# A two-block transformer forward pass: standardised tokens for router and experts, the norm's scale and bias applied elsewhere

## The chip, the cores and the metric

The kernel runs on one core of one Trainium2 chip. It is written in Bass: each engine has its own instruction stream, and semaphores order the streams. The time is the device time of one execution in microseconds (us), taken as the median of several runs. Lower is better.

## The reference

The program computes two blocks on 256 tokens of width 1024 in fp32. The first (retention, dilated attention, MLP) isn't touched. The second has two layers, and each ends so:

```python
heads = jnp.concatenate([y_a, y_b, y_c], -1)
mix = jnp.einsum('bsc,cd->bsd', heads, w_out[l])
x = _layernorm(DEEPNORM_ALPHA * x + mix, ln1_g[l], ln1_b[l])
ffn = _hier_moe(x, router_group_w[l], router_group_b[l], router_expert_w[l], router_expert_b[l],
                expert_w_gate[l], expert_w_up[l], expert_w_down[l])
x = _layernorm(DEEPNORM_ALPHA * x + ffn, ln2_g[l], ln2_b[l])
```

`_layernorm` subtracts the mean, multiplies by the inverse root of the variance, then by `g`, and adds `b`. The router (4 group logits, 16 expert logits per token, each a product with `x` plus a bias) picks one group and two of its four experts per token. An expert is silu(x w_gate) * (x w_up), weighted, then times w_down.

## The kernel before

Every large fp32 product is three fp32r products: ACT copies a weight unit (128x1024) rounded into `w_hi` (L660), GpSimd or VectorE subtracts to get `w_lo` (L604, L1894), activations are split likewise into `xT_hi`/`xT_lo`, `yT_hi`/`yT_lo`, `xg_hi`/`xg_lo`, and TensorE runs hi*hi, hi*lo, lo*hi (L1136 to L1138). Weights come by SyncE's DMAs into eight raw slots `w_raw`; four slots hold the split form. `unit_used`, `hi_ready` and `lo_ready` count units through these stages.

Each engine's order is written out by hand. In one layer, from the mixed heads on, it is this.

- **Head outputs.** TensorE turns pairs of head columns and multiplies by eight `w_out` units (`down_pairs`, `down_tail4`, L1228 and L1254). VectorE normalises the mLSTM heads in two halves (`centred`, L2558), then the SSD heads, and makes the `yT_lo` remainders (L1888). GpSimd splits the last four units in quarters (L604, 128x256 each), and then the router's unit (L646). `heads_wait` (L1748) holds the third and fourth turn until their heads are ready.
- **Norm.** VectorE adds each half of each 128-token tile (`residual`, L2328), takes statistics (L1930), and normalises in two passes per half (`normed`, L2293): `(x - mean) * g` into PSUM (L2298), then `* rstd + b` back to `x_sb` (L2301). `g` and `b` are rows broadcast to all partitions (`ln1_g`, `ln1_b` in `mod`). TensorE transposes the tile (`turn_x`, L1176), ACT and VectorE split it (L704, L1900).
- **Router.** 16 products of 40 and 20 columns per tile (L1768 to L1771) on the router's unit. VectorE adds the bias row (L2636) and picks groups and experts in a long row of dependent instructions on a few columns, each followed by a drain.
- **Gather.** ACT and VectorE split the normalised tokens untransposed (`xk_hi` L1067, `xk_lo` L2628). TensorE gathers them by one-hot products into four PSUM groups (L1798), transposed and sorted by expert group. ACT (L1072) and VectorE (L2699) split each group. In between VectorE makes `w_lo` of the first expert units, and behind the fourth group the routing weights (`comb`, L2706 to L2718).
- **Experts.** 16 visits. In the first TensorE takes three of four up units, then waits for `comb` (`route_in`) and multiplies it by the one-hots (L1847), and takes the fourth. ACT's silu (L1093) and VectorE's product with the weight (L2731) follow. GpSimd has no work in this stage.
- **Second residual.** VectorE adds the experts' sum to `x_sb` (L2768), so `x_sb` must hold the full normalised rows by then.

Layer 1 repeats this. Weight loads of the router's unit carry 160 columns of use and are padded to 1024.

## Time and profile before

| | us |
|---|---|
| median of 3 runs | 1416.35 |
| lowest, highest | 1414.29, 1416.54 |
| profiled execution, its time | 1416.86 |
| its span, first to last instruction | 1414.5 |
| PE / DVE / ACT / POOL busy | 1312.9 / 856.0 / 735.0 / 639.7 |

The profile is of one execution. Busy time is summed over instructions, and PE's instructions are pipelined, so its 93% isn't peak. DVE is VectorE, POOL is GpSimd, PE is TensorE. The chain follows back from the last instruction to whatever released each step. In a timeline, a bracket gives how long the engine sat idle before the row and whose instruction ended that. An instruction that was issued but had to wait inside its engine shows as a longer instruction, not as idle time.

### The profile page before, as it was taken

What the parts mean: (1) busy time and instruction counts of PE and PEld (TensorE: products, weight loads), DVE (VectorE), ACT (ScalarE), POOL (GpSimd) and SP (SyncE); (2) the same over time, 40 slices, a digit from 0 to 9 for tenths busy, and PEclk for the clock granted to TensorE, in tenths of its full rate; (3) what the DMA queues carried; (4) which work ended last, traced back from release to release, by engine and by line L of the source; (5) the groups of instructions that cost most, each with busy time, mean ns of one, the idle gap of its engine ahead of it and who ended that gap; (6) DMA issues with size and microseconds to landing.
All of it is one profiled execution on the core that took longest, in us unless ns stands there. A gap on an engine that the chain in (4) does not pass through costs nothing.

```text
span 1414.5 us, 17480 instructions
## 1 busy us (share of the span) xinstructions
PE 1312.9 (93%) x6096; PEld 1069.1 (76%) x6096; DVE 856.0 (61%) x1345; ACT 735.0 (52%) x1090; POOL 639.7 (45%) x522
## 2 busy tenths in 40 slices
PE   6899988999999899999998979999989988799996
PEld 3687767888886688887787767888868776788884
DVE  7574763354243543113677667878867857677777
ACT  4343443454464544445566426666646663467664
POOL 2899899988767789998400420000060024000000
PEclk9999999999999999999999879999999989799998
DMA  9966458665443545554531008878754300577782
GB/s 380 367 228 238 149 221 291 242 235 198 160 149 134 169 171 183 194 186 179 194 134 60 1 1 312 296 299 327 279 186 160 119 1 0 221 289 283 287 303 89
DMA packets 44476, 279.86 MB, mean 198 GB/s; under 512 B 5453, under 2 KB 8781, under 8 KB 12014
## 3 DMA queue, kind: packets, MB, share of 16 engines
q1 hardware_dynamic: 37426, 263.82, 50.9%
q10 hardware_dynamic: 6974, 15.05, 2.9%
q8 instruction: 44, 0.72, 0.2%
q14 instruction: 32, 0.26, 0.1%
HBM read 274.66 MB, written 4.19 MB: 197 GB/s over the span
## 4 chain that ended last, share of the span: by engine, by line
PE 69%; DVE 12%; POOL 10%; DVEq 3%; ACT 2%; issue 2%; DMA 2%; ACTq 0%; SPq 0%; POOLq 0%
PE G L1136 11%; PE G L1138 11%; PE G L1137 11%; POOL w_lo L604 10%; PE AC L1136 8%; PE AC L1138 8%; PE AC L1137 8%; DVE mod L1981 1%; DMA w_raw<-w_stream 1%; DVE w_lo L1894 1%; PE T L1251 1%; DVE arena L2481 1%; PE G L1708 1%; PE G L1700 1%; ACT w_hi L660 1%
## 5 line engine op out<-in xcount | busy, mean ns | idle before, releaser
L604 POOL TENSOR_TENSOR w_lo<-w_raw,w_hi 128x512 fp32r<-128x512 f32 (+1 forms) x480 | 612.6, 1309 | 365.8 <-ACT w_hi L660 357.9
L660 ACT ACTIVATE w_hi<-w_raw 128x1024 fp32r<-128x1024 f32 x448 | 470.6, 1056 | 395.1 <-PE G L1138 193.9
L1894 DVE TENSOR_TENSOR w_lo<-w_raw,w_hi 128x1024 fp32r<-128x1024 f32 x230 | 278.5, 1223 | 65.0 <-ACT w_hi L660 57.5
L1136 PE MATMUL AC<-w_hi,yT_hi 128*128 128x512 f32 x464 | 184.0, 397 | 3.4 <-DVE yT_lo L2738 1.9
L1136 PE MATMUL G<-w_hi,xT_hi 128*128 128x512 f32 x432 | 179.6, 416 | 1.9 <-DVE xT_lo L1900 1.9
L1137 PE MATMUL AC<-w_lo,yT_hi 128*128 128x512 f32 x464 | 181.2, 391 | 0.0
L1138 PE MATMUL AC<-w_hi,yT_lo 128*128 128x512 f32 x464 | 181.2, 390 | 0.0
L1137 PE MATMUL G<-w_lo,xT_hi 128*128 128x512 f32 x432 | 173.1, 401 | 0.0
L1138 PE MATMUL G<-w_hi,xT_lo 128*128 128x512 f32 x432 | 173.0, 400 | 0.0
L1136 PE MATMUL G<-w_hi,arena_r 128*128 128x512 f32 x320 | 128.0, 400 | 3.9 <-DVE arena L2731 3.4
L1138 PE MATMUL G<-w_hi,arena_r 128*128 128x512 f32 x320 | 125.1, 391 | 0.0
L1137 PE MATMUL G<-w_lo,arena_r 128*128 128x512 f32 x320 | 124.7, 390 | 0.0
L1981 DVE SCALAR_TENSOR_TENSOR mod<-w_raw,sm,mod 128x1024 f32<-128x1024 f32 x46 | 89.3, 1940 | 45.1 <-DMA w_raw<-w_stream 32.3
L1136 PE MATMUL AC<-w_hi,xT_hi 128*128 128x512 f32 x272 | 111.0, 408 | 5.6 <-POOL w_lo L604 5.5
L1138 PE MATMUL AC<-w_hi,xT_lo 128*128 128x512 f32 x272 | 106.3, 391 | 0.0
L1137 PE MATMUL AC<-w_lo,xT_hi 128*128 128x512 f32 x272 | 106.1, 390 | 0.0
L1136 PEld LDWEIGHTS AC<-w_hi,yT_hi 128*128 128x128 f32 x464 | 88.1, 190 | 23.4 <-POOL w_lo L604 3.2
L1138 PEld LDWEIGHTS AC<-w_hi,yT_lo 128*128 128x128 f32 x464 | 88.0, 190 | 18.5
L1137 PEld LDWEIGHTS AC<-w_lo,yT_hi 128*128 128x128 f32 x464 | 88.2, 190 | 17.4
L1136 PEld LDWEIGHTS G<-w_hi,xT_hi 128*128 128x128 f32 x432 | 84.2, 195 | 19.5 <-DVE xT_lo L1900 2.8
L1138 PEld LDWEIGHTS G<-w_hi,xT_lo 128*128 128x128 f32 x432 | 84.0, 194 | 18.7
L1137 PEld LDWEIGHTS G<-w_lo,xT_hi 128*128 128x128 f32 x432 | 84.4, 195 | 16.4 <-issue 0.2
(446 smaller groups left out, 1778.3 us busy)
## 6 DMA issues: line engine op xcount, KB each, us to landing
w_raw<-w_stream SPq DMA_DIRECT2D x152, 1024.0 KB, 4.9
w_raw<-w_expert SPq DMA_DIRECT2D x96, 1024.0 KB, 5.0
...
```

What stands on the lines that cost most here:

```text
L604: i = pool.tensor_tensor(w_lo[:, k % SLOTS, cols], w_raw[:, raw, cols], w_hi[:, k % SLOTS, cols].bitcast(F32), ALU.subtract)
L660: act.activation(w_hi[:, k % SLOTS, cols], w_raw[:, raw, cols], ACT.Copy).then_inc(hi_ready, 1)
L1136: pe.matmul(out, xh, wh, start=start, stop=False)
L1137: pe.matmul(out, xh, wl, start=False, stop=False)
L1138: return pe.matmul(out, xl, wh, start=False, stop=stop)
L1251: i = pe.transpose(T[:, t, c * P:(c + 1) * P], src[:, t, c * P:(c + 1) * P], ident[:, :])
L1700: i = pe.matmul(G[:, 0, c:c + LDH + 1], lw[:, (2 * h + d) % 4, st, t * P:(t + 1) * P], vaug[:, st, h, 0:LDH + 1], start=st == sts[0], stop ...
L1708: i = pe.matmul(G[:, 1, t * S + h * SP_:t * S + (h + 1) * SP_], sw[:, (2 * h + d) % 4, st, t * P:(t + 1) * P], xdt[:, st, d, h * SP_:(h + ...
L1894: dve.tensor_tensor(w_lo[:, k % SLOTS, :], w_raw[:, k % RAW, :], w_hi[:, k % SLOTS, :].bitcast(F32), ALU.subtract).then_inc(lo_ready, 1)
L1981: dve.scalar_tensor_tensor(m, w_raw[:, raw, :], csil[:, s:s + 1], m, ALU.mult, ALU.add).then_inc(ada_used, 1)
L2481: i = dve.scalar_tensor_tensor(xc[:, c, :], xpad[:, c, k:k + S], cv_w[:, c, k:k + 1], xc[:, c, :], ALU.mult, ALU.add)
```

## The change

- The `ln1_g` and `ln1_b` vectors are put in the router's unit as columns (8 + 8 columns behind the 160 weights). VectorE copies them to `gain_col`, `bias_col`, and multiplies the router's weights by the scale into columns 256 to 415 of the same raw slot; ACT and GpSimd split that.
- TensorE multiplies the broadcast bias column by the router's weights (eight fp32 products of 20 columns), and VectorE adds the result to the router's bias row (`r_bias`).
- The norm ends with one pass per half, `(x - mean) * rstd`. The four residual halves, statistics and `xT_lo` halves stand in a new order.
- TensorE transposes the first tile amid the last output product, and runs the first tile's second router half ahead of the second tile's transposes. ACT makes `xk_hi` of a tile right behind its transposed split.
- Each gathered group gets scale and bias by column: on ACT in the split (two instructions for one), on VectorE by two passes in place in PSUM before the remainder.
- GpSimd makes the full rows of `x_sb`, four instructions of 128x1024 per layer, released by the fourth gathered group's remainder (`t_lo`). The second residual waits for them (`x_full`).

```diff
@@ -148,6 +148,7 @@
 LN_ROWS = 4 * D
+SCALED = 256
@@ -414,6 +418,8 @@
         inv_row = sm[:, 436:452]
+        gain_col, bias_col = sm[:, 336:336 + KC], sm[:, 336 + KC:336 + 2 * KC]
+        r_bias = sm[:, 40:60]
         cosM = sm[:, 368:400].rearrange("p (t n) -> p t n", t=TOK)
@@ -643,8 +649,16 @@
                 pool.wait_ge(hi_ready, n + (L_ROUTER + 1))
-                pool.tensor_tensor(w_hi[:, s, ROUTER:2 * ROUTER], w_raw[:, raw_slot(n + L_ROUTER), 0:ROUTER],
+                pool.wait_ge(router_bias, l + 1)
+                pool.tensor_tensor(w_hi[:, s, ROUTER:2 * ROUTER], w_raw[:, raw_slot(n + L_ROUTER), SCALED:SCALED + ROUTER],
                                    w_hi[:, s, 0:ROUTER].bitcast(F32), ALU.subtract).then_inc(lo_ready, 1)
+
+                pool.wait_ge(ln_rows_loaded, l * 16 + 16)
+                pool.wait_ge(t_lo, l * LT + (T_LAYERS + LT_MOE + UP))
+                for t in range(TOK):
+                    pool.tensor_tensor(x_sb[:, t, :], x_sb[:, t, :], row2["ln1_g"], ALU.mult)
+                    pool.drain()
+                    pool.tensor_tensor(x_sb[:, t, :], x_sb[:, t, :], row2["ln1_b"], ALU.add).then_inc(x_full, 1)
@@ -656,8 +670,11 @@
                 act.wait_ge(unit_used, n + k + 1)
-                cols = slice(0, ROUTER if isinstance(n, int) and n >= U_LAYERS and (n + k - U_LAYERS) % L_UNITS == L_ROUTER else UNIT)
-                act.activation(w_hi[:, k % SLOTS, cols], w_raw[:, raw, cols], ACT.Copy).then_inc(hi_ready, 1)
+                if isinstance(n, int) and n >= U_LAYERS and (n + k - U_LAYERS) % L_UNITS == L_ROUTER:
+                    act.wait_ge(router_scaled, (n + k - U_LAYERS) // L_UNITS + 1)
+                    act.activation(w_hi[:, k % SLOTS, 0:ROUTER], w_raw[:, raw, SCALED:SCALED + ROUTER], ACT.Copy).then_inc(hi_ready, 1)
+                else:
+                    act.activation(w_hi[:, k % SLOTS, :], w_raw[:, raw, :], ACT.Copy).then_inc(hi_ready, 1)
@@ -1062,14 +1079,16 @@
                     turn_hi_x(t + (LT_X2 + 2 * tk), tk)
-                for tk in range(TOK):
                     act.wait_ge(x2_ready, HALVES * (l * TOK + (tk + 1)))
...
                     act.wait_ge(t_ready, t + (LT_MOE + q + 1))
-                    act.activation(xg_hi[:, 2 * q:2 * q + 2, :], AC[:, q, :].rearrange("p (c n) -> p c n", n=S), ACT.Copy).then_inc(t_hi, 1)
+                    for c in (2 * q, 2 * q + 1):
+                        i = act.activation(xg_hi[:, c, :], AC[:, q, c % 2 * S:(c % 2 + 1) * S], ACT.Identity, bias=bias_col[:, c:c + 1],
+                                           scale=gain_col[:, c:c + 1])
+                    i.then_inc(t_hi, 1)
@@ -1236,6 +1255,8 @@
                     for c in range(SLOTS):
+                        if j == 1 and c == 2:
+                            amid()
                         i = down_step(n, k, c, c, 1, (j,), False, c == SLOTS - 1)
@@ -1251,7 +1272,7 @@
-            def down_pairs(n, k, t, src, pairs, before=None, tail=True, tail4=False):
+            def down_pairs(n, k, t, src, pairs, before=None, tail=True, tail4=None):
@@ -1745,15 +1766,30 @@
+                def router_biases(c0, c1):
+
+                    raw = raw_slot(n + L_ROUTER)
+                    pe.wait_ge(raw_landed[raw // PIECE], (raw_round(n + L_ROUTER) + 1) * 16)
+                    for c in range(c0, c1):
+                        at = ROUTER + KC + c
+                        i = pe.matmul(G[:, 0, 0:ROUTER // KC], w_raw[:, raw, at:at + 1].to_broadcast([P, P]),
+                                      w_raw[:, raw, c * ROUTER // KC:(c + 1) * ROUTER // KC], start=c == 0, stop=c == KC - 1)
+                    return i
+
                 def heads_wait(q):
+                    if q == 2:
+                        pe.wait_ge(lnum_out, l * LH + LH)
+                        router_biases(0, KC // 2)
+                    if q == 3:
+                        router_biases(KC // 2, KC).then_inc(router_bias, 1)
                     if q >= 2:
...
-                down_pairs(n, L_OUT, tb + LT_OUT, lambda q: HB[:, :, q * 256:(q + 1) * 256], 4, heads_wait, tail4=True)
+                down_pairs(n, L_OUT, tb + LT_OUT, lambda q: HB[:, :, q * 256:(q + 1) * 256], 4, heads_wait,
+                           tail4=lambda: turn_x(tb + LT_X2, 0, x_sb, x2_ready, HALVES * l * TOK))
...
-                turn_x(tb + LT_X2, 0, x_sb, x2_ready, HALVES * l * TOK)
                 pe.wait_ge(lo_ready, n + (L_ROUTER + 1))
@@ -1774,8 +1810,8 @@
                 pe.wait_ge(t_lo, tb + (LT_X2 + 2))
+                router(0, range(KC // 2, KC))
                 turn_x(tb + (LT_X2 + 2), 1, x_sb, x2_ready, HALVES * (l * TOK + 1))
-                router(0, range(KC // 2, KC))
                 pe.wait_ge(t_lo, tb + (LT_X2 + 3))
@@ -2586,6 +2622,12 @@
                 down_los(tb + LT_OUT, 0, 1)
+                raw = raw_slot(n + L_ROUTER)
+                dve.wait_ge(raw_landed[raw // PIECE], (raw_round(n + L_ROUTER) + 1) * 16)
+                dve.tensor_copy(sm[:, 336:336 + 2 * KC], w_raw[:, raw, ROUTER:ROUTER + 2 * KC])
+                dve.tensor_tensor(w_raw[:, raw, SCALED:SCALED + ROUTER].rearrange("p (c n) -> p c n", c=KC),
+                                  w_raw[:, raw, 0:ROUTER].rearrange("p (c n) -> p c n", c=KC),
+                                  w_raw[:, raw, ROUTER:ROUTER + KC].unsqueeze(2).to_broadcast([P, KC, ROUTER // KC]), ALU.mult).then_inc(router_scaled, 1)
                 centred(2, LH)
@@ -2614,26 +2656,41 @@
                 down_los(tb + LT_OUT, 2, 4)
-                for t in range(TOK):
+                dve.wait_ge(router_bias, l + 1)
+                dve.tensor_tensor(r_bias, G[:, 0, 0:ROUTER // KC], row2["router_b"], ALU.add)
+
+                def summed(t, c):
+                    acc_wait(l * LACC + ACC_LAYERS, n + done(L_ROUTER), t, c)
+                    residual(t, c)
+                    stats_half(t, c)
+
+                def standard(t):
+
+                    inverse_root(r + 4 + t, t)
                     for c in range(HALVES):
-                        acc_wait(l * LACC + ACC_LAYERS, n + done(L_ROUTER), t, c)
-                        residual(t, c)
-                        stats_half(t, c)
-                    ln_var(t)
-                    if t == 0:
-                        dve.wait_ge(ln_rows_loaded, l * 16 + 16)
-                    normed(r + 4 + t, t, "ln1_g", "ln1_b", x2_ready, (lambda: lo_x(tb + LT_X2, 0)) if t == 1 else None)
+                        dve.tensor_scalar(x_sb[:, t, half(c)], x_sb[:, t, half(c)], mv[:, t, 0:1], var[t], ALU.subtract, ALU.mult).then_inc(x2_ready, 1)
+
+                summed(0, 0)
+                summed(0, 1)
+                ln_var(0)
+                standard(0)
+                summed(1, 0)
+                lo_x_half(tb + LT_X2, 0, 0)
+                summed(1, 1)
+                ln_var(1)
+                lo_x_half(tb + LT_X2, 0, 1)
+                standard(1)
                 def token_lo(t):
...
+                token_lo(0)
                 lo_x(tb + (LT_X2 + 2), 1)
-                token_lo(0)
                 token_lo(1)
...
                 nr = EGROUPS + EXPERTS
-                dve.tensor_tensor(rlog, AC[:, 0:TOK, 0:nr], wide(row2["router_b"]), ALU.add)
+                dve.tensor_tensor(rlog, AC[:, 0:TOK, 0:nr], wide(r_bias), ALU.add)
                 dep()
@@ -2696,6 +2753,10 @@
                     dve.wait_ge(t_hi, tb + (LT_MOE + q + 1))
+                    for c in (2 * q, 2 * q + 1):
+                        gathered = AC[:, q, c % 2 * S:(c % 2 + 1) * S]
+                        dve.tensor_scalar(gathered, gathered, gain_col[:, c:c + 1], bias_col[:, c:c + 1], ALU.mult, ALU.add)
+                    dep()
                     dve.tensor_tensor(xg_lo[:, 2 * q:2 * q + 2, :], AC[:, q, :].rearrange("p (c n) -> p c n", n=S),
@@ -2765,6 +2826,7 @@
                         dve.wait_ge(acc_ready, l * LACC + (ACC_LAYERS + 3 + HALVES * t + c + 1))
+                        dve.wait_ge(x_full, l * TOK + t + 1)
                         residual(t, c)
@@ -2830,7 +2892,9 @@
         router = np.concatenate([a["router_group_w_2"][l], we], axis=1)
-        parts.append(padded(router.reshape(KC, P, -1).transpose(1, 0, 2).reshape(1, P, -1), UNIT))
+        affine = np.concatenate([a[k][l].reshape(KC, P).T for k in ("ln1_g_2", "ln1_b_2")], axis=1)
+        router = np.concatenate([router.reshape(KC, P, -1).transpose(1, 0, 2).reshape(P, -1), affine], axis=1)
+        parts.append(padded(router[None], UNIT))
     units = np.concatenate(parts, axis=0).reshape(-1, RAW, P, UNIT)
```

VectorE's order in the norm, before (`x_sb` the tokens, `sm` the statistics, `AC` and `T` PSUM):

```order
L2298 SCALAR_TENSOR_TENSOR AC<-x_sb,sm,mod 128x512 x2
L1947 RECIPROCAL sm<-sm 128x1
L2301 SCALAR_TENSOR_TENSOR x_sb<-AC,sm,mod 128x512 x2
L2328 SCALAR_TENSOR_TENSOR x_sb<-x_sb,AC 128x512
L1930 BN_STATS sm<-x_sb 128x6
L2328 SCALAR_TENSOR_TENSOR x_sb<-x_sb,AC 128x512
L1930 BN_STATS sm<-x_sb 128x6
L1935 BN_AGGR sm<-sm 128x2
L2333 TENSOR_SCALAR sm<-sm 128x1
L1900 TENSOR_TENSOR xT_lo<-T,xT_hi 128x4x128 x2
```

and now:

```order
L2369 TENSOR_SCALAR sm<-sm 128x1
L1983 RECIPROCAL sm<-sm 128x1
L2671 TENSOR_SCALAR x_sb<-x_sb,sm 128x512 x2
L2364 SCALAR_TENSOR_TENSOR x_sb<-x_sb,AC 128x512
L1966 BN_STATS sm<-x_sb 128x6
L1936 TENSOR_TENSOR xT_lo<-T,xT_hi 128x4x128
L2364 SCALAR_TENSOR_TENSOR x_sb<-x_sb,AC 128x512
L1966 BN_STATS sm<-x_sb 128x6
L1971 BN_AGGR sm<-sm 128x2
L2369 TENSOR_SCALAR sm<-sm 128x1
L1936 TENSOR_TENSOR xT_lo<-T,xT_hi 128x4x128
```

Two passes per tile through PSUM are one pass in place, and the first tile's `xT_lo` halves stand apart, the first of them ahead of the second tile's last residual.

VectorE's order behind the second gathered group, before (`w_lo<-w_raw,w_hi` an expert unit's remainder, `arena_r<-AC` a group's, `sm` the routing weights):

```order
L2699 TENSOR_TENSOR arena_r<-AC,arena_r 128x512
L1894 TENSOR_TENSOR w_lo<-w_raw,w_hi 128x1024
L2699 TENSOR_TENSOR arena_r<-AC,arena_r 128x512
L1894 TENSOR_TENSOR w_lo<-w_raw,w_hi 128x1024 x2
L2706 TENSOR_REDUCE sm<-sm 128x2
L2707 TENSOR_SCALAR sm<-sm 128x2
L2709 TENSOR_TENSOR sm<-sm 128x2
L2711 RECIPROCAL sm<-sm 128x2
L2712 TENSOR_TENSOR sm<-sm 128x8
L2714 TENSOR_TENSOR sm<-sm 128x8
L2716 TENSOR_TENSOR sm<-sm 128x8
L2718 TENSOR_TENSOR sm<-sm 128x32
```

and now:

```order
L1930 TENSOR_TENSOR w_lo<-w_raw,w_hi 128x1024
L2758 TENSOR_SCALAR AC<-AC,sm 128x256 x2
L2760 TENSOR_TENSOR arena_r<-AC,arena_r 128x512
L1930 TENSOR_TENSOR w_lo<-w_raw,w_hi 128x1024
L2758 TENSOR_SCALAR AC<-AC,sm 128x256 x2
L2760 TENSOR_TENSOR arena_r<-AC,arena_r 128x512
L1930 TENSOR_TENSOR w_lo<-w_raw,w_hi 128x1024 x2
L2767 TENSOR_REDUCE sm<-sm 128x2
L2768 TENSOR_SCALAR sm<-sm 128x2
L2770 TENSOR_TENSOR sm<-sm 128x2
L2772 RECIPROCAL sm<-sm 128x2
L2773 TENSOR_TENSOR sm<-sm 128x8
```

A pair of scalar passes stands ahead of each group's remainder; the units and the routing weights follow as before.

GpSimd's order at the same place, before:

```order
L639 TENSOR_TENSOR arena<-arena 128x256 x2
L639 TENSOR_TENSOR arena<-arena 128x128 x2
L639 TENSOR_TENSOR arena<-arena 128x256
L604 TENSOR_TENSOR w_lo<-w_raw,w_hi 128x256 x16
L646 TENSOR_TENSOR w_hi<-w_raw,w_hi 128x160
L604 TENSOR_TENSOR w_lo<-w_raw,w_hi 128x256 x32
```

and now:

```order
L610 TENSOR_TENSOR w_lo<-w_raw,w_hi 128x256 x16
L653 TENSOR_TENSOR w_hi<-w_raw,w_hi 128x160
L659 TENSOR_TENSOR x_sb<-x_sb,mod 128x1024
L661 TENSOR_TENSOR x_sb<-x_sb,mod 128x1024
L659 TENSOR_TENSOR x_sb<-x_sb,mod 128x1024
L661 TENSOR_TENSOR x_sb<-x_sb,mod 128x1024
L610 TENSOR_TENSOR w_lo<-w_raw,w_hi 128x256 x32
```

Between the router's unit and the next layer's first eight units stand four instructions on whole rows.

## Rows read from the trace of the kernel before

**Rows 1.** Page: busy us (share) xinstructions; the chain that ended last, by engine.

```profile
PE 1312.9 (93%) x6096; PEld 1069.1 (76%) x6096; DVE 856.0 (61%) x1345; ACT 735.0 (52%) x1090; POOL 639.7 (45%) x522
...
PE 69%; DVE 12%; POOL 10%; DVEq 3%; ACT 2%; issue 2%; DMA 2%; ACTq 0%; SPq 0%; POOLq 0%
```

**Rows 2.** VectorE timeline: start, duration (us), engine, line, out<-in, xcount [idle before].

```profile
800.10 0.85 DVE L1888 TENSOR_TENSOR yT_lo<-T,yT_hi 128x256 fp32r<-128x256 f32 x2 [2.97 <-ACT yT_hi L672]
...
801.62 0.76 DVE L2571 TENSOR_TENSOR arena<-arena,sm 128x256 f32<-128x256 f32 x2
...
805.87 0.17 DVE L1916 TENSOR_SCALAR sm<-sm 128x8 f32<-128x8 f32 x1
```

**Rows 3.** Timeline of GpSimd, then of TensorE, the output product's stretch.

```profile
807.38 13.93 POOL L604 TENSOR_TENSOR w_lo<-w_raw,w_hi 128x256 fp32r<-128x256 f32 x16 [13.60 <-ACT w_hi L660]
...
809.25 0.66 PE L1251 MATMUL T<-ident,arena 128*128 128x128 f32 x4 [1.17 <-DVE arena L2599]
...
821.37 0.50 PE L1136 MATMUL AC<-w_hi,yT_hi 128*128 128x512 f32 x1 [0.23 <-POOL w_lo L604]
```

**Rows 4.** Timeline of VectorE, norm of both tiles and router.

```profile
825.61 1.41 DVE L2298 SCALAR_TENSOR_TENSOR AC<-x_sb,sm,mod 128x512 f32<-128x512 f32 x2
...
830.59 0.69 DVE L1930 BATCH_NORM_STATS2 sm<-x_sb 128x6 f32<-128x512 f32 x1
...
831.71 1.28 DVE L1900 TENSOR_TENSOR xT_lo<-T,xT_hi 128x512 fp32r<-128x512 f32 x2
...
834.46 1.41 DVE L2301 SCALAR_TENSOR_TENSOR x_sb<-AC,sm,mod 128x512 f32<-128x512 f32 x2
...
842.24 0.20 DVE L2636 TENSOR_TENSOR sm<-AC,mod 128x40 f32<-128x40 f32 x1 [1.00 <-PE AC L1771]
```

**Rows 5.** Timeline of TensorE: small fp32 products, then the turning of both tiles.

```profile
780.08 1.45 PE L1708 MATMUL G<-arena 128*128 128x64 f32 x12
...
828.31 1.03 PE L1176 MATMUL T<-ident,x_sb 128*128 128x128 f32 x8
...
835.32 1.94 PE L1176 MATMUL T<-ident,x_sb 128*128 128x128 f32 x8 [1.74 <-issue]
```

**Rows 6.** Windows: stretch, us, busy by engine, granted clock, DMA share, GB/s.

```profile
834.00:836.00 2.00, 0.69 (x4) 0.72 (x5) 1.80 (x4) 0.00 (x0) 0.00 (x0) 0.55 0.00 0
854.00:855.00 1.00, 1.00 (x8) 1.00 (x8) 0.74 (x2) 0.90 (x2) 0.00 (x0) 0.66 0.97 410
```

**Rows 7.** VectorE groups by shape: line, op, shapes xcount | busy us, mean ns.

```profile
L2679 DVE TENSOR_SCALAR xT_lo<-arena,sm 128x256 fp32r<-128x256 f32 x4 | 1.2, 350 | 0.2
...
L2421 DVE COPY arena<-arena 128x512 f32<-128x512 f32 x2 | 0.9, 428 | 0.1
```

**Rows 8.** Timeline of VectorE, then of TensorE: gather and first visit.

```profile
854.87 1.23 DVE L1894 TENSOR_TENSOR w_lo<-w_raw,w_hi 128x1024 fp32r<-128x1024 f32 x1 [0.26 <-ACT w_hi L660]
...
861.95 0.19 DVE L2718 TENSOR_TENSOR sm<-sm 128x32 f32<-128x32 f32 x1
...
864.44 0.96 PE L1847 MATMUL T<-sm,xT_lo 128*128 128x16 f32 x8
...
870.33 0.47 PE L1136 MATMUL G<-w_hi,arena_r 128*128 128x512 f32 x1 [1.69 <-DVE arena L2731]
```

**Rows 9.** Timeline of GpSimd at 509 and 1051 us, of VectorE at 522 and 814.

```profile
509.82 13.52 POOL L604 TENSOR_TENSOR w_lo<-w_raw,w_hi 128x512 fp32r<-128x512 f32 x10 [0.17 <-ACT w_hi L660]
524.35 2.55 POOL L604 TENSOR_TENSOR w_lo<-w_raw,w_hi 128x512 fp32r<-128x512 f32 x2 [1.00 <-ACT w_hi L660]
...
1051.81 11.38 POOL L604 TENSOR_TENSOR w_lo<-w_raw,w_hi 128x256 fp32r<-128x256 f32 x16 [6.04 <-ACT w_hi L660]
...
522.22 1.18 DVE L2267 SCALAR_TENSOR_TENSOR sm<-sm 128x32 f32<-128x32 f32 x1
523.47 0.18 DVE L2269 TENSOR_SCALAR sm<-sm 128x32 f32<-128x32 f32 x1
...
814.02 0.69 DVE L2612 TENSOR_TENSOR arena<-arena,sm 128x512 f32<-128x512 f32 x1
```

7 lines of the change are left out of this document (5 added, 2 removed).

## The prediction

> **What bounds the kernel now.** I read the page first. TensorE (PE) is busy 93% of the span and carries 69% of the chain that ended last; VectorE (DVE) and GpSimd (POOL) carry 12% and 10% [rows 1]. The change touches only the two layers of the second block, so I read the timelines of layer 0 from 799 to 872 us, engine by engine; layer 1 shows the same rows 368.4 us later. Three stretches matter.
>
> *Head outputs.* DVE runs without a gap from 800.1 us to the variance of 805.87 [rows 2]. The ACT root waits for that, the conversion of the next weights stands behind the root, POOL's sixteen pieces wait for the conversion and start at 807.38, and PE waits 0.23 us for them at 821.37 [rows 3]. So a delay of DVE here passes to PE.
>
> *Norm and router.* DVE spends 1.41 us on each of two passes per tile [rows 4]. PE ends the output product near 828.3 and then mostly waits: it turns the first tile at 828.31, the second only at 835.32 [rows 5], and DVE gets the router's logits at 842.24 [rows 4]. The granted clock is 1.00 (2.4 GHz) until inside 834 to 836 us (0.55 there), and is back only inside 854 to 855 us, some 5 us after PE's work became dense again at 849.5 [rows 6]. The fall comes about 5 us after the dense products ended; layer 1 does the same.
>
> *Gather and first visit.* DVE is still choosing experts when the first gathered group is ready, and PE's first expert product waits for DVE's unit of 854.87. The routing weights are ready at 862.14 (861.95 plus 0.19), PE asks for them at 864.44 and has passed on by then; PE next waits at 870.33, for DVE's hidden product [rows 8]. From about 875 us to the end of the stage PE is full, so any delay up to there stays.
>
> **The change, part by part, for one layer.**
>
> 1. Two DVE instructions for the router unit: a copy of 16 columns and a product of 160. They stand in the DVE run above. Two 256-column products take 0.76 us together [rows 2], 0.38 for each step; 160 columns come to about 0.28, the copy to 0.08. Bounds 0.2 and 0.6; I take **+0.35 us**, all on the path.
>
> 2. Eight small matmuls for the bias on PE, four before the third turn and four before the fourth. PE is idle for 1.17 us before the third turn [rows 3] and nearly as long before the fourth, and both gaps grow by 0.35. Six fp32 products of 64 columns take 1.45 us at full clock (12 records [rows 5]), 0.24 each; these have 20 columns, so four take at most 0.97: **0**. If that cover were gone they would cost up to 1.7. The 20-column addition of the bias lies in DVE's wait before 822.4: 0.
>
> 3. The norm. Four passes of 0.7 us per tile and half (1.41 and 1.41 per tile [rows 4]) become one scalar-pair pass per half. No 512-column pass with two scalar columns shows alone. The nearest rows are a 512-column copy within SBUF of 0.43 us and a 256-column scalar pass of 0.35 [rows 7]; the passes of now, 0.7, are the other end. I take 0.54, which is 0.35 plus the extra columns at the copy's pace, and 0.45 per step. The Trainium skill ("VectorE: DVE Perf Modes", Mode 2×_2P) lets a one-source fp32 pass within SBUF move two elements a cycle, and the copy's 0.43 us agrees; by it alone the pass is 0.43, and the sum changes by 0.2 us.
>
>    Tile 0 is then standardised at 827.2, in time for PE, which turns it between two products. That adds 1.0 us of transposes before PE's last product: its end moves from 828.3 to about 829.5. DVE's last half then goes: residual and statistics 1.45 (0.75 and 0.7 [rows 4]), aggregation and variance 0.5, one xT_lo half 0.6 (two take 1.28), reciprocal 0.2, two passes 1.0, giving 833.2 instead of 835.87 (834.46 plus 1.41). PE has done the first tile's router products by then. It turns tile 1 by 834.0, still at full clock by the fall seen [rows 6]. ACT and DVE need 1.1 to 1.6 more; the sixteen router products at half clock need 3.4. The logits come at about 838.65 instead of 842.24: -3.6, and with the 0.35 above **-3.2 us**. Bounds: -1.8 (clock falls before the transposes) and -5.3 (it stays up through the router). The token copies and remainders hide beside PE.
>
> 4. The gather. On DVE each of four groups gets two 256-column passes on PSUM, near 0.37 a step like the pairs of 0.75 to 0.85 [rows 2]: +0.75 each. The first unit for PE is ready 0.9 us later (two groups, less some 0.6 of waits for ACT that vanish, 0.26 of it before the unit [rows 8]), and the fourth group is done 2.6 us later. ACT's two halves in place of one cost 0.15 each and hide. **+0.9 us** if nothing else happens: the weights would be ready at 864.75 and PE would ask at 865.3.
>
> 5. POOL's full rows: four products and sums of 128x1024, released by DVE's fourth group, at about 861.05. POOL is free until the next layer, so its own time costs nothing. What it does to DVE is the main term. In rows 9, ten POOL instructions of 512 columns run back to back from 509.82 to 523.34. Beside them dependent DVE instructions on 32 columns take 1.17 us each; when POOL stops, the same instruction takes 0.18 (523.47). So a DVE instruction that reads two SBUF tensors, or passes SBUF to SBUF with scalars, waits for one whole POOL instruction, and the two engines alternate. This agrees with the Trainium skill ("SBUF — State Buffer", which calls the shared port pair an exclusive lock, held for the whole instruction).
>
>    The new instructions are four times as wide as the 256-column ones. 256 columns take 0.71 us and 512 take 1.275 [rows 9], 0.565 per 256, so 1024 take 2.4 us. Bounds of the hold: 1.3 (no longer than 512 columns) and 2.7. Behind POOL's start DVE has in its queue the third and fourth w_lo units and the eight tiny weight instructions. After the third unit POOL gets in four times: before the fourth unit, and before three of the tiny ones. I take 9.2 us of waits: weights at 864.75 + 9.2 = 873.95. The three last tiny steps run free, included in that.
>
>    **Who waits:** PE stands between the third and fourth unit of the first visit until the weights come. It would have gone on at 864.44; now at 873.95: **+9.5 us** (this contains the 0.9 of point 4; the slack of 0.55 is used up). PE was then idle for 8.7 us, more than the 5 us after which the clock fell, and comes back at half clock for some 5 us, as at 849.5 [rows 6]. That costs up to 2.4 us before the hidden product. I take **+2.0**. DVE's next three units and ACT's silu are ready beside that. From there PE is the limit again and nothing is given back.
>
> 6. The wait for the full rows before the second residual is some 150 us later: 0. The other moves (ACT's token copies, tile 1 turned behind the router products) are inside point 3.
>
> Sum for one layer: -3.2 + 9.5 + 2.0 = +8.3 us; for two +16.6. Against the profiled execution (1416.86 us, its span 1414.5) that is 1433.5. The median of the runs is 0.5 lower, so I say **1433 us**.
>
> **The rivals.**
>
> *A, the row work hides (faster).* If DVE and POOL do not exclude each other here, only points 1 to 4 count: -3.2 + 0.9 = -2.3 a layer, -4.6 in all, **1411.8 us**. For it: POOL has no other work then, and one product with a broadcast operand (814.02) ran at its usual 0.69 us while POOL worked. Against it: the tiny instructions of rows 9 are of the very kinds that stand in this queue. It decides by whether the fourth group's successors lengthen.
>
> *B, the other order of turns.* DVE gets both w_lo units through before POOL's first instruction. Then one turn of POOL falls behind the weights: weights at 871.5, then DVE's next unit waits, and the hidden product comes 9.5 us late instead of 11.5. -3.2 + 9.5 = +6.3, **1429.0 us**. Against it: the paired rows at full load show POOL coming in between.
>
> *C, half the holds.* If POOL holds 1.3 us for each turn, or only two turns fall before the weights, they cost about 4.8 instead of 9.2 us and PE's idle time is too short to lower the clock for long: 9.5 - 4.4 = +5.1, less 3.2, +1.9 a layer, **1420 us**. With the clock also kept up in the router it is zero to slightly faster.
>
> *D, the clock stays up through the router.* PE has router products until 830.5 and again from 832.1, more than before, so the fall may come later. Point 3 is then -5.3; with the holds in place +6.2 a layer, **1429 us**.
>
> **How the numbers follow.** About 0.2% (2.8 us) is what a measurement of this kernel tells from none. Main course 0.48, B 0.14, D 0.10, all slower; C 0.15, of which 0.07 slower, 0.06 within and 0.02 faster; A 0.13, of which 0.12 faster and 0.01 within. Slower 0.79, same 0.07, faster 0.14. The top of the range is a hold of 2.7 us for each of four turns and the whole 2.4 for the clock: about +11.5 a layer, 1439. The bottom leaves out A and the faster part of C: 1415. Between them lies some 0.83.
>
> **What the profile of the changed kernel would show.** DVE's w_lo unit behind the fourth group at 2.5 to 3.5 us instead of 1.22, and two or three of the tiny weight instructions at 2.3 us instead of 0.17 (point 5). POOL's four row instructions at 2.4 us or a little more, spread over 10 to 12 us. A wait of PE of 8 to 9 us before the small products for the weights, with a granted clock of 0.50 after it. In the norm, passes of 0.43 to 0.7 us, logits 3 us earlier counted from PE's last head product, and PE's wait for POOL there unchanged near 0.2. I am wrong if the w_lo units stay at 1.22 while POOL works: then it is A. I am wrong in size if the holds are much shorter than 2.4 us, or if PE's stall is there and the clock is not lowered.

## The result

Over six runs each the changed kernel takes 1432.78 us (median) against 1414.51 us before, a ratio of 1.0137 with a 95% interval of 1.0115 to 1.0159: slower by 19.4 us (16.3 to 22.5). The forecast was 1433.

The page of the changed kernel, busy time and chain by engine, as [rows 1]:

```profile
PE 1321.5 (92%) x6128; PEld 1075.8 (75%) x6128; DVE 866.8 (60%) x1359; ACT 737.7 (51%) x1098; POOL 662.1 (46%) x530
...
PE 67%; DVE 13%; POOL 10%; DVEq 3%; ACT 2%; DMA 2%; issue 2%; SPq 0%; ACTq 0%; POOLq 0%
```

TensorE's share of the chain falls by two points though it has a little more to do: it waits. Three rows of its timeline in layer 0 show where. The first is its first expert product. The second is the place: it answers to the row at 864.44 in [rows 8]. The third answers to 870.33 there:

```profile
857.23 0.50 PE L1155 MATMUL G<-w_hi,arena_r 128*128 128x512 f32 x1 [1.43 <-DVE w_lo L1930]
...
873.96 1.89 PE L1883 MATMUL T<-sm,xT_lo 128*128 128x16 f32 x8 [8.07 <-DVE sm L2779]
...
882.27 0.47 PE L1155 MATMUL G<-w_hi,arena_r 128*128 128x512 f32 x1 [1.69 <-DVE arena L2792]
```

What VectorE does meanwhile (timeline, columns as in [rows 2]), and GpSimd's four new instructions:

```profile
859.91 1.00 DVE L2758 TENSOR_SCALAR AC<-AC,sm 128x256 f32<-128x256 f32 x2
860.99 0.69 DVE L2760 TENSOR_TENSOR arena_r<-AC,arena_r 128x512 fp32r<-128x512 f32 x1
861.59 4.55 DVE L1930 TENSOR_TENSOR w_lo<-w_raw,w_hi 128x1024 fp32r<-128x1024 f32 x2
866.07 0.15 DVE L2767 TENSOR_REDUCE sm<-sm 128x2 f32<-128x8 f32 x1
866.14 2.24 DVE L2768 TENSOR_SCALAR sm<-sm 128x2 f32<-128x2 f32 x1
868.45 2.21 DVE L2770 TENSOR_TENSOR sm<-sm 128x2 f32<-128x2 f32 x1
870.74 0.17 DVE L2772 RECIPROCAL sm<-sm 128x2 f32<-128x2 f32 x1
870.82 2.32 DVE L2773 TENSOR_TENSOR sm<-sm 128x8 f32<-128x8 f32 x1
873.22 0.17 DVE L2775 TENSOR_TENSOR sm<-sm 128x8 f32<-128x8 f32 x1
...
861.82 3.24 POOL L659 TENSOR_TENSOR x_sb<-x_sb,mod 128x1024 f32<-128x1024 f32 x1 [31.98 <-DVE arena_r L2760]
865.21 3.14 POOL L661 TENSOR_TENSOR x_sb<-x_sb,mod 128x1024 f32<-128x1024 f32 x1
868.32 2.33 POOL L659 TENSOR_TENSOR x_sb<-x_sb,mod 128x1024 f32<-128x1024 f32 x1
870.79 2.34 POOL L661 TENSOR_TENSOR x_sb<-x_sb,mod 128x1024 f32<-128x1024 f32 x1
```

An addition to two columns (L2768) takes 2.24 us, and a product of two columns (L2770) 2.21, thirteen times the 0.17 of the reciprocal behind it. The two engines take turns: DVE's second unit waits for POOL's first instruction, and three tiny DVE instructions each wait for one of the others. The reduction does not wait, though POOL is at work beside it (866.07). The reciprocal (870.74) falls where POOL passes from its third instruction to its fourth, so whether it would wait is not shown.

The norm, second tile (timelines of VectorE and TensorE, as [rows 4] and [rows 5]):

```profile
834.36 1.00 DVE L2671 TENSOR_SCALAR x_sb<-x_sb,sm 128x512 f32<-128x512 f32 x2
...
841.93 0.20 DVE L2693 TENSOR_TENSOR sm<-AC,sm 128x40 f32<-128x40 f32 x1 [1.36 <-PE AC L1807]
...
835.76 1.97 PE L1195 MATMUL T<-ident,x_sb 128*128 128x128 f32 x8
```

Windows of the changed kernel, in the norm and in the wait and restart (columns as in [rows 6]):

```profile
834.00:836.00 2.00, 1.74 (x9) 1.74 (x10) 1.92 (x5) 0.00 (x0) 0.00 (x0) 0.64 0.00 0
870.00:872.00 2.00, 0.00 (x0) 0.00 (x0) 1.93 (x3) 0.00 (x0) 1.86 (x2) 0.50 0.23 94
878.00:880.00 2.00, 2.00 (x9) 1.59 (x8) 0.00 (x0) 0.00 (x0) 0.00 (x0) 0.77 0.89 377
```

The two rows of the kernel before from which I count, first residual and first gather instruction on VectorE, and the latter of the changed kernel:

```profile
822.37 0.69 DVE L2328 SCALAR_TENSOR_TENSOR x_sb<-x_sb,AC 128x512 f32<-128x512 f32 x1 [4.41 <-PE AC L1138]
...
852.92 0.69 DVE L2699 TENSOR_TENSOR arena_r<-AC,arena_r 128x512 fp32r<-128x512 f32 x1
```

```profile
852.60 0.55 DVE L2758 TENSOR_SCALAR AC<-AC,sm 128x256 f32<-128x256 f32 x1
```

To compare kernels I measure the stage from starts of rows, so that nothing ahead of it enters: from VectorE's first residual to the logits (the 128x40 addition), from there to the first gather instruction on VectorE, and from that one to three points: TensorE's first expert product, the end of the routing weights, and VectorE's hidden product of the first visit. Microseconds, layer 0 / layer 1:

| kernel | residual to logits | logits to gather | gather to first product | to weights | to hidden |
|---|---|---|---|---|---|
| before | 19.87 / 19.87 | 10.68 / 10.66 | 3.23 / 3.24 | 9.22 / 9.22 | 16.39 / 16.39 |
| after | 17.31 / 17.07 | 10.67 / 10.62 | 4.63 / 4.64 | 21.30 / 21.30 | 28.65 / 28.92 |
| one column | 16.29 / 17.54 | 10.67 / 10.62 | 4.63 / 4.64 | 12.78 / 12.79 | 17.99 / 19.40 |
| before plus rows | 19.86 / 19.86 | 10.69 / 10.33 | 3.23 / 2.94 | 17.59 / 17.50 | 25.23 / 25.31 |
| rows late | 17.56 / 17.03 | 10.65 / 10.61 | 4.64 / 4.64 | 12.78 / 12.78 | 17.99 / 17.99 |
| quarters | 16.27 / 16.28 | 10.66 / 10.62 | 4.64 / 4.63 | 15.46 / 15.48 | 23.67 / 20.74 |
| dense wait | 17.54 / 16.29 | 10.67 / 10.62 | 4.64 / 4.63 | 21.47 / 21.44 | 26.82 / 26.77 |
| late, dense norm | 14.64 / 14.64 | 10.67 / 10.62 | 4.63 / 4.64 | 12.77 / 12.78 | 17.96 / 18.01 |
| late, plain gather | 16.30 / 17.55 | 10.67 / 10.31 | 3.24 / 3.23 | 9.22 / 9.22 | 16.43 / 16.40 |
| gather reordered | 15.82 / 14.65 | 10.66 / 10.61 | 2.95 / 2.96 | 12.78 / 12.78 | 19.41 / 19.39 |
| before, dense norm | 18.10 / 18.11 | 10.69 / 10.65 | 3.23 / 3.13 | 9.22 / 9.12 | 16.44 / 16.33 |
| before, all edits | 18.11 / 18.10 | 10.69 / 10.65 | 2.28 / 2.63 | 9.23 / 9.58 | 14.54 / 14.81 |
| before, fills | 19.86 / 19.86 | 10.69 / 10.66 | 3.13 / 3.05 | 10.53 / 10.46 | 16.29 / 16.21 |
| unit 3 first | 14.63 / 14.64 | 10.68 / 10.62 | 2.96 / 2.96 | 12.78 / 12.79 | 16.38 / 16.39 |

(With one column, layer 1 reads 19.40: the clock fell right behind the wait ahead of the first product there, at about 1218.9, and was back at 1222.)

From residual to hidden product a layer is 46.94 us before and 56.63 after: +9.69, and +0.34 in the heads ahead of it, so about 20 us in two layers. That is the measured difference, within its interval. The profiled execution itself took 1438.42 us, the slowest of the six, and its span is 22.1 us longer than the one before; the other 2 us stand almost all ahead of layer 0's heads (800.10 before, 802.01 after), in code that the change doesn't touch.

### The profile page after: what moved, and what is told of

It reads as the page before. It is cut to its first block, busy times and chain, and to the rows that moved or that the text cites. A ratio compares the mean times of both kernels' runs of the same rounds, so it can differ in the third digit from the quotient of the medians.

```text
span 1436.6 us, 17600 instructions
## 1 busy us (share of the span) xinstructions
PE 1321.5 (92%) x6128; PEld 1075.8 (75%) x6128; DVE 866.8 (60%) x1359; ACT 737.7 (51%) x1098; POOL 662.1 (46%) x530
## 4 chain that ended last, share of the span: by engine, by line
PE 67%; DVE 13%; POOL 10%; DVEq 3%; ACT 2%; DMA 2%; issue 2%; SPq 0%; ACTq 0%; POOLq 0%
PE G L1155 11%; PE G L1157 10%; PE G L1156 10%; POOL w_lo L610 10%; PE AC L1155 8%; PE AC L1157 8%; PE AC L1156 8%; DMA w_raw<-w_stream 2%; DVE mod L2017 2%; DVE w_lo L1930 1%; PE T L1272 1%; DVE arena L2517 1%; PE G L1721 1%; PE AC L1616 1%; PE G L1729 1%
## 5 line engine op out<-in xcount | busy, mean ns | idle before, releaser
L1930 DVE TENSOR_TENSOR w_lo<-w_raw,w_hi 128x1024 fp32r<-128x1024 f32 x230 | 282.5, 1242 | 61.9 <-ACT w_hi L677 54.3
L2017 DVE SCALAR_TENSOR_TENSOR mod<-w_raw,sm,mod 128x1024 f32<-128x1024 f32 x46 | 82.1, 1784 | 42.2 <-DMA w_raw<-w_stream 32.8
```

What stands on the lines that cost most here:

```text
L1930: dve.tensor_tensor(w_lo[:, k % SLOTS, :], w_raw[:, k % RAW, :], w_hi[:, k % SLOTS, :].bitcast(F32), ALU.subtract).then_inc(lo_ready, 1)
L2017: dve.scalar_tensor_tensor(m, w_raw[:, raw, :], csil[:, s:s + 1], m, ALU.mult, ALU.add).then_inc(ada_used, 1)
```

## Experiments

Time differences are the measured ratio times the median of the kernel before in the same call, with the 95% interval.

**One column.** Is it GpSimd's work, or the new arithmetic?

```diff
-pool.tensor_tensor(x_sb[:, t, :], x_sb[:, t, :], row2["ln1_g"], ALU.mult)
+pool.tensor_tensor(x_sb[:, t, 0:1], x_sb[:, t, 0:1], row2["ln1_g"][:, 0:1], ALU.mult)
...
```

The addition behind it is cut to one column in the same way.

> The changed kernel, with GpSimd's four row instructions of a layer cut from 1024 columns to one; the scale and bias of the other columns of the residual rows are left out of the computation. Everything else of the change stays. Theory (VectorE and GpSimd wait for each other's whole instructions at the router's end): VectorE's waits of 2.35 us fall away, the expert weights are ready about 9 us earlier, TensorE's clock stays up. Left over are +0.34 (heads), -2.56 (norm and router) and about +1.4 (gather) a layer, so -0.8 a layer: about 1413 us, between -4 and +1 us against the kernel before. Rival (the new gather, the two scalings or the normalisation cost the time themselves and GpSimd's work is beside it): the time stays above 1425 us, at least +10 us against before.

Measured: -0.6 us (-4.9 to +3.7). The row that took 2.24 us is gone from VectorE's timeline, and GpSimd's instructions wait in turn for VectorE's (1.03 us for one column, 0.19 once VectorE's wide units are over). Timelines of this kernel:

```profile
859.20 0.16 DVE L2768 TENSOR_SCALAR sm<-sm 128x2 f32<-128x2 f32 x1
...
857.09 1.03 POOL L659 TENSOR_TENSOR x_sb<-x_sb,mod 128x1 f32<-128x1 f32 x1 [30.95 <-DVE arena_r L2760]
...
859.22 0.19 POOL L659 TENSOR_TENSOR x_sb<-x_sb,mod 128x1 f32<-128x1 f32 x1
```

All of the loss goes with the width of those four instructions.

**The same instructions in the kernel before**, with nothing else of the change:

```diff
+for t in range(TOK):
+    pool.tensor_tensor(HB[:, t, :], x_sb[:, t, :], row2["ln1_g"], ALU.mult)
+    pool.drain()
+    pool.tensor_tensor(HB[:, t, :], HB[:, t, :], row2["ln1_b"], ALU.add).then_inc(x_full, 1)
...
```

> The kernel before, with four GpSimd instructions of 128x1024 a layer at the place where the changed kernel has them; their results go to scratch and are used by nobody. Nothing else of the change is in it. Lock theory: four waits of 2.3 us on VectorE put the expert weights 9.2 us later, at 871.3 on the scale of the first layer, of which TensorE had 2.3 in hand (864.44), so 6.9 us of stall, and about 2.4 us for a TensorE clock that falls in the stall: about +9.3 a layer, +18.5 in all, 1433 us. Rival (the loss of the changed kernel is in its gather and norm): within 2 us of the kernel before.

Measured: +18.4 us (10.4 to 26.3). Weights 8.37 us later, hidden product 8.84. VectorE and TensorE there:

```profile
853.69 4.57 DVE L1902 TENSOR_TENSOR w_lo<-w_raw,w_hi 128x1024 fp32r<-128x1024 f32 x2
...
858.25 2.27 DVE L2715 TENSOR_SCALAR sm<-sm 128x2 f32<-128x2 f32 x1
...
865.91 1.89 PE L1855 MATMUL T<-sm,xT_lo 128*128 128x16 f32 x8 [5.95 <-DVE sm L2726]
```

So the four instructions are enough by themselves. That both kernels lose the same by them, while the rest of the change nets to nothing, is what these two runs show together.

**Quarters.** Does a wait last as long as one instruction?

```diff
+for a in range(0, D, D // 4):
+    pool.tensor_tensor(x_sb[:, t, a:a + D // 4], x_sb[:, t, a:a + D // 4], row2["ln1_g"][:, a:a + D // 4], ALU.mult)
...
```

> The changed kernel with each GpSimd row instruction cut in four of 256 columns, same place, same amount of work. If a VectorE instruction waits for one whole GpSimd instruction and the two take turns: seven to eight short VectorE instructions wait 0.6 to 0.7 us each, 4.6 us in the place of 9.2, and the clock falls for a shorter time: 1420 to 1424 us. If the wait is for all of GpSimd's work in a row (it does not let VectorE in between), it stays at 1431 to 1435 us. If the holds are shorter than GpSimd's gaps, under 1418 us.

Measured: +7.5 us (3.4 to 11.7), 1421.29. The same DVE rows as above, of this kernel:

```profile
856.02 2.90 DVE L1933 TENSOR_TENSOR w_lo<-w_raw,w_hi 128x1024 fp32r<-128x1024 f32 x2
...
858.90 0.63 DVE L2771 TENSOR_SCALAR sm<-sm 128x2 f32<-128x2 f32 x1
```

The waits are 0.4 to 0.55 us in place of 2.1: they shrink with the length of one GpSimd instruction. Six waits put the weights 2.7 us later than with the rows late, less than the 4.6 expected: presumably part of a GpSimd instruction's 0.7 us has passed when VectorE asks. In layer 0 TensorE waited 2.24 us for the weights and the clock fell behind that (0.50 from 863 to 869 us). In layer 1, where the clock had fallen earlier and slowed the first products, it waited 0.82 us and the clock stayed up until 1241.7, behind the hidden product. So it is 23.67 against 20.74 us to the hidden product, for the same 15.5 to the weights: 2.9 us for where the clock falls.

**Dense wait.** What is the clock's part? TensorE fills its wait with 36 products into a bank that nobody reads; "dense products" below are such products too.

```diff
+pe.wait_ge(lo_ready, n + (L_MOE + UP))
+for spare in range(36):
+    pe.matmul(T[:, 1, :], xg_hi[:, 0, 0:P], w_hi[:, (L_MOE + UP - 1) % SLOTS, 0:NT], start=True, stop=True)
 pe.wait_ge(route_in, l * 4 + 4)
```

> The changed kernel, with 36 products of 128x512 on TensorE (into a bank that nobody reads) at the place where it waits for the expert weights, 36 x 0.23 = 8.3 us, so that the wait of 8.07 us is filled and the clock does not fall in it. The wait itself stays. If the clock's fall costs what the forecast said (2.0 to 2.4 us a layer), the time is 4 to 5 us below the changed kernel's, 1427 to 1429 us. If the clock costs nothing on the path (rival: VectorE's three operands at 874 to 877 and ScalarE set the pace of the restart), it stays within 1 us of the changed kernel's +19 us over before.

Measured: 1428.22 us, +15.1 (9.5 to 20.8) over before. The intervals of this run and of the changed kernel overlap, so the stage decides: hidden product after 26.82 / 26.77 instead of 28.65 / 28.92, that is 1.8 and 2.15 us less, although the spare products hold TensorE 0.5 us longer than the weights do (they are ready at 868.61, TensorE goes on at 869.08). With that 0.5 the clock's fall costs 2.3 and 2.6 us. The products on TensorE:

```profile
860.75 8.50 PE L1882 MATMUL T<-w_hi,arena_r 128*128 128x512 f32 x36 [0.33 <-DVE w_lo L1933]
```

The window behind the wait is at 1.00 here. In the changed kernel, which runs 5.7 us later by its first residual, the clock is at 0.50 from 869 to 878 us, in the wait and behind it:

```profile
870.00:872.00 2.00, 2.00 (x13) 1.70 (x13) 2.00 (x3) 0.00 (x0) 0.00 (x0) 1.00 0.00 0
```

**Rows late.** GpSimd's rows behind hidden tiles of the visits, one at a time:

```diff
 for t in range(TOK):
+    pool.wait_ge(ffn_h, l * VISITS + FF_TILES + 4 * t + 4)
     pool.tensor_tensor(x_sb[:, t, :], x_sb[:, t, :], row2["ln1_g"], ALU.mult)
     pool.drain()
+    pool.wait_ge(ffn_h, l * VISITS + FF_TILES + 4 * t + 6)
```

> The changed kernel with the same four GpSimd instructions moved behind the expert products, one behind every second hidden tile of the visits, where VectorE has idle time. The full computation. Theory: in the visits VectorE is waited for with room, so each 2.3 us hold is hidden, and the time is that of the kernel with one column: about 1413 us, -4 to +1 us against before. Rival (a hold costs wherever it falls, since VectorE's accumulations are needed in time by TensorE there too): four holds of 2.3 us a layer, up to +9 us a layer, 1420 to 1432 us.

Measured: +0.7 us (-3.2 to +4.7). The hold is still there: four units of VectorE take 6.84 us where a row of four without GpSimd takes 5.10 (at 885.28), and nobody waits for them. Timelines of VectorE and GpSimd:

```profile
893.69 6.84 DVE L1932 TENSOR_TENSOR w_lo<-w_raw,w_hi 128x1024 fp32r<-128x1024 f32 x4
...
893.90 3.28 POOL L660 TENSOR_TENSOR x_sb<-x_sb,mod 128x1024 f32<-128x1024 f32 x1 [69.35 <-DVE arena L2794]
```

**Late rows, plain gather**: the above with the gather of before.

```diff
-for c in (2 * q, 2 * q + 1):
-    gathered = AC[:, q, c % 2 * S:(c % 2 + 1) * S]
-    dve.tensor_scalar(gathered, gathered, gain_col[:, c:c + 1], bias_col[:, c:c + 1], ALU.mult, ALU.add)
...
```

> The changed kernel with GpSimd's rows late, and with the gather of the kernel before: the scale and bias of the gathered rows are left out of the computation (one copy on ScalarE, no scaling on VectorE). It measures the gather alone, and by what is left the gain of norm and router. Theory: the gather cost +1.4 us a layer, norm and router gave -2.2 together with the heads: about 3 us below the run with the rows late, 4.4 us below before, 1408 to 1411 us. Rival (the gather's extra VectorE work hides behind TensorE, whose first product waits for something else): same as with the rows late, 1413 us.

Measured: -4.1 us (-6.5 to -1.6). The scale and bias of the gathered rows are left out here. The three columns behind the first gather instruction return to those of before, to 0.04 us. So the new gather costs 1.40 us to the first product and 1.6 to the hidden product, and what norm and router gain is real.

**Late rows, dense norm.** Eight dense products between the two halves of the first tile's router:

```diff
 router(0, range(KC // 2))
+for spare in range(8):
+    pe.matmul(G[:, 1, :], xT_hi[:, 0, 0:P], w_hi[:, (L_OUT + 5) % SLOTS, 0:NT], start=True, stop=True)
```

> The changed kernel with GpSimd's rows behind the visits (as in the run with the rows late) and 8 products of 128x512 on TensorE into a bank that nobody reads, in its wait of 1.7 us between the two halves of the first tile's router products, so that the clock stays at 1.0 for the second tile's transposes and the last router products. In the changed kernel these ran at 0.5: the transposes took 1.97 instead of 1.03 us, and from the last products' start to the logits it was 3.64 us, of which some 1.5 are the half clock. Theory: 1.5 to 2.4 us a layer less than with the rows late alone, -3 to -5 us in all, 1408 to 1411 us. Rival (VectorE's chain of rests and token remainders ends last there, not TensorE): no difference from the rows late alone.

Measured: -7.2 us (-10.3 to -4.0) against before, 1408.27 us. Residual to logits is 14.64 in both layers. The products on TensorE:

```profile
828.76 2.08 PE L1815 MATMUL G<-w_hi,xT_hi 128*128 128x512 f32 x8
```

This kernel's first residual comes 3.7 us earlier than the changed kernel's, so the window that stood at 0.64 there is 830.31 to 832.31 here. It and the window of the last router products:

```profile
830.31:832.31 2.00, 2.00 (x18) 1.82 (x17) 1.92 (x5) 0.12 (x1) 0.00 (x0) 1.00 0.00 0
834.00:836.00 2.00, 1.53 (x14) 1.43 (x13) 1.70 (x4) 0.23 (x1) 0.00 (x0) 1.00 0.00 0
```

**Before, dense norm**: 12 such products ahead of the first tile's router products and 7 behind their first half, in the kernel before.

> The kernel before with only dense products on TensorE (into a bank that nobody reads): 12 in its wait of 3.2 us ahead of the first tile's router products, 7 in its wait of 1.7 us ahead of the second tile's transposes. It tells whether the gain of the dense products belongs to the changed kernel or to any kernel with this norm. In the kernel before the clock fell to 0.5 during the second tile's transposes: they took 1.94 instead of 1.03 us, and the last products ran at half clock. Theory: the clock stays up, 1.5 to 2.5 us a layer less, 1409 to 1411 us, so that the kernel before with it stands within 3 us of the changed kernel with rows late and dense products. Rival (in the kernel before VectorE's remainders of the tokens, L2628, and not TensorE end last there): no gain, 1414 us.

Measured: -5.0 us (-7.4 to -2.5), 1409.67 us; residual to logits 18.10 / 18.11 instead of 19.87. So the kernel before gets 5.0 us by them too, where the changed arithmetic with them and the late rows stands at -7.2. The stage accounts for 3.5 of the 5.0; where the rest lies is not shown.

**Gather reordered.** Unit 0 ahead of the second group:

```diff
 gathered(0)
+his(L_MOE, L_MOE + 1, n)
 gathered(1)
-his(L_MOE, L_MOE + 1, n)
...
-if q:
-    unit_lo(n, L_MOE + q - 1)
+unit_lo(n, L_MOE + q)
```

> The kernel with GpSimd's rows late and dense products in the norm, and with the first expert unit brought forward: ScalarE makes the rounded copy of expert unit 0 ahead of the second gathered group, and VectorE makes the remainder of unit q right behind group q instead of behind group q+1. The full computation. With the rows late TensorE waited 1.60 us for that first remainder, and then ran its 36 products without a stop while VectorE needed 2.8 us for each group and unit, as long as TensorE's 12 products. Theory: TensorE starts 1.5 to 1.8 us earlier and stays ahead, since each later group is due exactly when VectorE has it: -3 us in all against the kernel without the reordering, 1404 to 1406 us. Rival (what is won at the start comes back as waits for groups 1 to 3 or for the expert weights, VectorE being the bound of the whole stretch): no difference, 1408 us.

Measured: -3.3 us (-5.2 to -1.4) against before: no better than without it, against what was expected. TensorE starts 1.7 us earlier and then waits 1.24 us for the weights, which VectorE has no sooner; the clock falls behind that wait, and the hidden product is 1.4 us later. In layer 0 the clock also fell within the last router products (at 832.4), in spite of the dense products: 15.82 us to the logits for 14.65. TensorE:

```profile
858.57 1.06 PE L1887 MATMUL T<-sm,xT_lo 128*128 128x16 f32 x8 [1.24 <-DVE sm L2781]
```

The window behind it:

```profile
860.00:862.00 2.00, 2.00 (x7) 1.61 (x6) 2.00 (x3) 0.00 (x0) 0.00 (x0) 0.50 0.92 315
```

**Unit 3 first.** `visit_up(0, range(UP))` ahead of the weights, so that nothing waits for them:

> The kernel with the gather reordered, and on TensorE the products of expert unit 3 put ahead of the 12 small ones that wait for the expert weights. The full computation. In the run before this one TensorE began its expert products 2.18 us earlier (848.69 against 850.87), then waited 1.24 us for the weights, its clock fell to 0.5 right after that wait, and unit 3 ran at half speed: 0.95 us later at the first SiLU than without the reordering. Theory (that wait with the clock's fall is what gave the gain back): with unit 3 in front of it there is no wait, the clock stays up, and the first SiLU comes some 3 us earlier a layer; of it VectorE's three remainders ahead of the hidden tile leave about 2: 1402 to 1405 us. Rival (VectorE's row of remainders sets the pace of the first visit whatever TensorE does): no better than 1408 us.

Measured: -6.9 us (-10.2 to -3.5), 1408.57. The stage is now 1.6 us a layer shorter than with the dense norm alone (hidden after 16.38 instead of 17.96), the time is the same. The clock, up until then, falls in the next wait, which was there before too. TensorE, layer 0:

```profile
864.46 0.70 PE L1157 MATMUL G<-w_hi,arena_r 128*128 128x512 f32 x1 [1.66 <-DVE arena L2793]
```

Windows:

```profile
864.00:866.00 2.00, 1.54 (x4) 1.28 (x5) 1.45 (x2) 0.00 (x0) 0.00 (x0) 0.63 0.87 369
866.00:868.00 2.00, 2.00 (x9) 1.60 (x8) 0.00 (x0) 0.60 (x1) 0.00 (x0) 0.51 0.94 254
```

Layer 1 does the same: a wait of 1.71 us at 1229.98, and 0.50 in the window from 1230 to 1232. In the kernel with the dense norm alone that wait had 1.69 us too, and the clock stayed up. The half-speed products give back what the stage had won: from the first residual to the hidden product of the second visit it is 51.44 us with the dense norm alone and 51.45 here (layer 1: 51.43 and 51.32), and TensorE has no other wait in between in either kernel.

**Before, all edits**: the three edits in the kernel before.

> The kernel before (the norm with its four passes, plain gather, no rows on GpSimd) with the three edits found on the way: dense products in the norm, unit 0 brought forward in the gather, unit 3 ahead of the weights. It tells what the changed arithmetic is worth once both kernels have them. Its gather on TensorE ended only 0.3 us before the first expert product, so bringing unit 0 forward wins little here. Theory (the changed arithmetic gains 2.2 us a layer in heads, norm and router and loses up to 1.4 in the gather): 0 to 4 us above the kernel with unit 3 first. Rival (the plain gather leaves VectorE free, and the first visit becomes faster here): as fast or faster than it.

Measured: -5.5 us (-8.6 to -2.5), 1408.43. It stands level with the changed arithmetic. Its norm is 3.5 us a layer slower (18.11), its gather and first visit 1.6 to 1.8 faster, so by the table it should be some 3 us behind. In the profiles the rest of layer 0 makes up for nearly all of that (321.15 us here, 323.87 with unit 3 first), and the medians do not resolve it.

**GpSimd that only writes**, in the kernel before: six zero fills of 128x2048 a layer.

> The kernel before, with six GpSimd instructions a layer at the same place that only write: 128x2048 of zeros into scratch that nobody reads. Nothing else of the change. It tells what kind of GpSimd work holds VectorE up. If any GpSimd instruction holds VectorE for its whole duration: holds at each of the small instructions of the router's end, and at least +10 us. If only one that reads two operands does: within 3 us of before.

Measured: -3.1 us (-5.8 to -0.3), no loss. VectorE was held once (timelines of GpSimd and VectorE):

```profile
854.84 11.46 POOL L651 MEMSET arena<- 128x2048 f32 x6 [30.92 <-DVE arena_r L2704]
...
857.03 1.58 DVE L2712 TENSOR_SCALAR sm<-sm 128x2 f32<-128x2 f32 x1
858.68 0.17 DVE L2714 TENSOR_TENSOR sm<-sm 128x2 f32<-128x2 f32 x1
```

A fill takes 1.91 us; the scalar instruction waited until the second ended (854.84 plus two fills is 858.66). The products of two SBUF tensors around it, which waited for GpSimd's additions, went at their usual 0.17 beside the fills. The Trainium skill ("SBUF — State Buffer", section "Who interferes with whom") says the same: an instruction with two SBUF inputs contends only with a GpSimd instruction that reads SBUF, one in a two-port mode with any, a reduction with none. The rows of this run and of the changed kernel agree in all three, if the scalar instruction that waited (1.58 us) runs in such a mode, which no row shows; the reductions took 0.15 and 0.16 us beside an addition and beside a fill.

## Why the prediction was right, and where it was not

*The mechanism (point 5) held.* The forecast named four turns of GpSimd of 2.3 us ahead of the weights, one before the fourth unit and three at tiny instructions. The rows show those: 2.20 (4.55 less 2.35), 2.09, 2.04 and 2.17, in all 8.50 for the forecast's 9.2. The weights were forecast 21.03 us behind the first gather instruction (873.95 less 852.92), and came after 21.30.

*TensorE's wait:* from that instruction to the small products it took 11.52 before (864.44 less 852.92) and takes 21.36: +9.8, forecast 9.5. *The clock:* from there to the hidden product's release 5.89 before and 8.31 now, +2.4, where I took 2.0 of "up to 2.4". The dense wait isolates it at 2.3 and 2.6.

*The gather (point 4) was mis-sized.* I took 0.75 us for a pair of scalar passes on PSUM, from pairs of two-tensor products; they take 1.00 (859.91), and the first product is 1.40 us later instead of 0.9. The weights without GpSimd come 3.56 us later, not 2.6. This and the smaller holds cancel in the weights.

*The norm (point 3) failed in one step.* The two passes take 1.00 us together, as assumed. But "It turns tile 1 by 834.0, still at full clock by the fall seen" did not hold in the profiled run. TensorE was ready for the turn in time (835.76, on a scale that by then stands 2.25 us later than before), but the clock had fallen at about 834.6, 10.0 us behind the first residual, and the transposes took 1.97. The forecast took the fall from the one trace at hand, where it comes 11.8 us behind the first residual. The gain was 2.56 and 2.80 instead of 3.6.

The other traces show that this moment is not fixed. With the changed norm and no dense products it lies between 9.1 and 12.2 us behind the first residual. Where it comes behind the start of the second tile's transposes, residual to logits is 16.27 to 16.30 (five layers in the table), 3.57 to 3.60 less than before: the forecast's case. Where it comes within the second half of the first tile's router products, it is 17.0 to 17.3; ahead of them, or with the first of them, 17.54 to 17.56, which with the heads' 0.34 is a gain of 2.0, near the bound of 1.8. Where it never falls it is 14.64, 5.2 less, or 4.9 with the heads: near the bound of 5.3, which rival D had.

In the kernel before it wanders as much, and nothing comes of it. With the rows added there it fell 9.4 us behind the first residual, in its own trace 11.8, and residual to logits is 19.86 and 19.87: TensorE turns the second tile only at 12.95, behind either. The change moved TensorE's work into the stretch in which the clock falls. Windows of the kernel before plus rows, whose first residual is at 817.71:

```profile
826.20:826.70 0.50, 0.00 (x0) 0.00 (x0) 0.43 (x2) 0.00 (x0) 0.00 (x0) 1.00 0.00 0
827.20:827.70 0.50, 0.00 (x0) 0.00 (x0) 0.50 (x2) 0.17 (x1) 0.00 (x0) 0.50 0.00 0
```

*The heads:* 0.17 and 0.32 us for the two new instructions; TensorE's wait for GpSimd stayed at 0.24, and the way from the heads' first row to it grew by 0.34, for 0.35. The bias matmuls (point 2; 0.96 us for four, forecast at most 0.97) and the wait for the full rows (point 6) cost nothing that shows.

*The sum* was 8.3 a layer; the stage shows 10.0. The median was hit all the same because a second error went the other way: 16.6 was set on a kernel before of 1416.35, whose median over six runs is 1414.51. The medians differ by 18.3, so the sum was 1.7 too small and its base 1.8 too high. That the forecast came within 0.2 us is luck; what the terms earn is an error of about 2 us.

*The rivals:* A (no exclusion) fell with the first trace, and its price, 1411.8, is what the runs without the holds give: 1411.69 and 1413.20. B fell by the order of the rows. C, half the holds, is nearest to what quartering does: 1421.29, forecast 1420; but the parts differ (2.7 us of waits for the 4.8, and a clock that did fall in layer 0), so the agreement is partly luck too. D happened in no layer without dense products. The top of the range does not follow from the two terms it names: four holds of 2.7 us and 2.4 for the clock come to +10.3 a layer, 1437, not +11.5 and 1439.
